# W3 of the experts in three fp32r passes throughout, with a full high part and moved inner buffers

## What is computed

```python
def hier_moe(h, w_rg, b_rg, w_re, b_re, w1, w3, w2):
    ...  # comb: weights of the two chosen experts of each token
    for g in range(N_EXPERT_GROUPS):
        a = jnp.einsum('btd,edf->btef', h, w1[g])
        b = jnp.einsum('btd,edf->btef', h, w3[g])
        hid = jax.nn.silu(a) * b * comb[:, :, g, :, None]
        out = out + jnp.einsum('btef,efd->btd', hid, w2[g])
    return out
```

## Time and profile before

| | |
|---|---|
| median of three executions | 1249.23 us (1248.32 to 1250.2) |
| the profiled execution | 1248.79 us, its span 1246.9 us |
| PE busy | 1164.0 us, 93% of the span |
| DVE busy | 706.2 us, 57% |
| ACT busy | 530.7 us, 44% |
| DMA, mean | 281 GB/s |
| experts: L1182, passes, 512 columns | 128 of each kind, 392 to 402 ns each |
| experts: L1210, fp32 products, 256 columns | 256 records (two for a product), 379 ns each, 60.5 us |
| experts: `e2Lo` splits | 32 (two in each of the 16 tiles), 2290 ns each |

### The profile page before, as it was taken

How to read it: one execution, slowest core, us unless ns; L and a number is a source line. 1 busy time by engine, 2 the same in 40 slices (tenths; PEclk the granted TensorE clock), 3 DMA queues, 4 the chain that set the end, 5 groups by cost and what they waited for, 6 DMA issues and landing times. The chain is left out here.

```text
span 1246.9 us, 21908 instructions
## 1 busy us (share of the span) xinstructions
PE 1164.0 (93%) x8635; PEld 1000.1 (80%) x8635; DVE 706.2 (57%) x1189; ACT 530.7 (43%) x744; POOL 175.1 (14%) x277
## 2 busy tenths in 40 slices
PE   3789999999999999999999999999499999999966
PEld 2678889888898998996779999998477777777742
DVE  1544655565656545553344443568777777777736
ACT  5323333232423323331244444334267676677632
POOL 0054344344443000000000000000300000000011
PEclk9799999999999999999979999999699999999997
DMA  9999878769656598648798786492599999999815
GB/s 299 322 376 354 287 265 309 272 222 319 235 171 239 202 344 280 253 154 325 278 333 292 274 282 224 122 339 70 193 353 409 404 381 376 377 367 378 314 55 190
DMA packets 172797, 350.37 MB, mean 281 GB/s; under 512 B 11347, under 2 KB 110187, under 8 KB 170630
## 3 DMA queue, kind: packets, MB, share of 16 engines
q1 hardware_dynamic: 164198, 326.35, 73.1%
q0 software_dynamic: 6304, 14.50, 3.4%
q10 hardware_dynamic: 2224, 8.52, 2.1%
HBM read 319.78 MB, written 117.65 MB: 351 GB/s over the span
## 5 line engine op out<-in xcount | busy, mean ns | idle before, releaser
L844 PE MATMUL psum<-hHi,whi 128*128 128x272 f32 x1216 | 360.8, 297 | 3.8 <-ACT rb L1378 2.0
L844 PE MATMUL psum<-hLo,whi 128*128 128x272 f32 x1216 | 353.2, 290 | 0.0
L844 PE MATMUL psum<-hHi,wlo 128*128 128x272 f32 x1216 | 351.7, 289 | 0.0
L844 PEld LDWEIGHTS psum<-hHi,whi 128*128 128x128 f32 x1216 | 231.1, 190 | 21.6 <-issue 17.8
L844 PEld LDWEIGHTS psum<-hHi,wlo 128*128 128x128 f32 x1216 | 231.2, 190 | 0.0
L844 PEld LDWEIGHTS psum<-hLo,whi 128*128 128x128 f32 x1216 | 230.7, 190 | 0.0
L1543 DVE TENSOR_TENSOR wlo<-wraw,whi 128x1024 fp32r<-128x1024 f32 x100 | 131.4, 1317 | 68.9 <-ACT whi L1292 68.4
L1292 ACT ACTIVATE whi<-wraw 128x1024 fp32r<-128x1024 f32 x100 | 104.7, 1051 | 27.0 <-PE psum L844 21.5
L2058 DVE TENSOR_TENSOR e2Lo<-e,e2Hi 128x2048 fp32r<-128x2048 f32 x32 | 73.3, 2290 | 32.7 <-ACT e2Hi L1468 31.8
L1378 ACT ACTIVATE rb<-psum 128x272 f32<-128x272 f32 x48 | 18.9, 394 | 136.7 <-PE psum L844 127.8
L2058 DVE TENSOR_TENSOR e1Lo<-e,e1Hi 128x2048 fp32r<-128x2048 f32 x30 | 68.6, 2285 | 5.7 <-ACT e1Hi L1477 4.2
(11 more groups left out here) (351 smaller groups left out, 2303.1 us busy)
## 6 DMA issues: line engine op xcount, KB each, us to landing
e<-in_w_dram SPq DMA_DIRECT2D x48, 2048.0 KB, 10.9
wraw<-in_w_in_dram SPq DMA_DIRECT2D x76, 512.0 KB, 5.1
out_dram<-in_cache_k_dram SPq DMA_DIRECT2D x32, 1022.0 KB, 8.8
out_dram<-in_cache_v_dram SPq DMA_DIRECT2D x32, 1022.0 KB, 8.0
adar<-in_w_ada_dram SPq DMA_DIRECT2D x36, 512.0 KB, 6.1
kvr<-in_cache_k_dram SPq DMA_DIRECT2D x8, 2048.0 KB, 9.4
kvr<-in_cache_v_dram SPq DMA_DIRECT2D x8, 2048.0 KB, 8.2
out_dram<-in_cache_k_dram SPq DMA_DIRECT2D x8, 1016.0 KB, 6.7
```

Source lines behind the costliest of these rows:

```text
L844: mm = pe.matmul(psum[:, t, 0:HALF], w[:, slot, k, :], x[:, k, cols], start=(k == 0 and n == 0), stop=(k == k_n - 1 and n == 2))
```

## The change

- The high part `e3Hi` gets eight blocks instead of four. ACT fills it in two copies of four blocks, one after the other, where there was one, for the first tile and in every tile's loop body.
- DVE makes `e3Lo` in two splits: both behind `xgLo` in the loop, the second one behind `xgLo` and ahead of `e2Lo` at the start. The copy to `xg32` goes, and the buffer too.
- PE makes all of B by passes: 24 of 256 columns in each half, and waits for the second split of `e3Lo` at k = 4 of half 0. The transposes of the hidden rows keep their place between k = 3 and k = 4 of half 1.
- `lo_done` and `hi_done` get six counts in a tile, so 10 becomes 12 and 5 becomes 6 in the waits.
- `sil`, `hid` and `hidHi` lie at the start of memory, where tables of the conditioning (`small` to `A2`) were; `xgHi` lies behind `xgLo`, which makes room for the larger `e3Hi`. ACT's first `e3Hi` therefore waits for `moved_act`.

```diff
@@ buffers
     e2Hi = r("e2Hi", [P, FC, D], F32R)
     xgLo = r("xgLo", [P, 2, KC, TS], F32R)
+    xgHi = r("xgHi", [P, 2, KC, TS], F32R)
+    assert r.at <= x2_at
+    r = Region(base + P * 4)
     sil = r("sil", [TS, DE])
     hid = r("hid", [TS, DE])
     hidHi = r("hidHi", [P, FC, TS], F32R)
-    assert r.at <= x2_at
+    assert r.at <= last2_at
...
-    e3Hi = r("e3Hi", [P, KC // 2, DE], F32R)
-    xgHi = r("xgHi", [P, 2, KC, TS], F32R)
-    xg32 = r("xg32", [P, 2, KC // 2, TS])
+    e3Hi = r("e3Hi", [P, KC, DE], F32R)
@@ PE
-                        pe.wait_ge(lo_done, 10 * jp + (SPLIT + 5 * q + 2 + k // 4))
+                        pe.wait_ge(lo_done, 12 * jp + (SPLIT + 6 * q + 2 + k // 4))
...
-                    for k in range(KC // 2):
-                        if half == 0 and k == 0:
-                            pe.wait_ge(lo_done, 10 * jp + (SPLIT + 5 * q + 4))
-                        passes(out, xgHi[:, q, k, :], xgLo[:, q, k, :], e3Hi[:, k, cols], e3Lo[q][:, k, cols],
-                               k == 0, False)
-                    if half == 1:
-                        pe.wait_ge(hid_done, 4 * jp + (2 * q + 3))
-                        hidden_T(0, 3)
-                    for k in range(KC // 2, KC):
-                        mm = pe.matmul(out, xg32[:, q, k - KC // 2, :], e3[q][:, k, cols], start=False,
-                                       stop=(k == KC - 1))
+                    for k in range(KC):
+                        if half == 0 and k % 4 == 0:
+                            pe.wait_ge(lo_done, 12 * jp + (SPLIT + 6 * q + 4 + k // 4))
+                        if half == 1 and k == KC // 2:
+                            pe.wait_ge(hid_done, 4 * jp + (2 * q + 3))
+                            hidden_T(0, 3)
+                        mm = passes(out, xgHi[:, q, k, :], xgLo[:, q, k, :], e3Hi[:, k, cols], e3Lo[q][:, k, cols],
+                                    k == 0, k == KC - 1)
                     mm.then_inc(b_pe, 1)
@@ ACT, ahead of the loop
             act.wait_ge(e3_in[0], 16)
-            act.activation(e3Hi[:, :, :], e3[0][:, 0:4, :], ACT.Copy).then_inc(hi_done, 1)
+            act.wait_ge(moved_act, 3)
+            for ks in (slice(0, 4), slice(4, 8)):
+                act.activation(e3Hi[:, ks, :], e3[0][:, ks, :], ACT.Copy).then_inc(hi_done, 1)
             act.wait_ge(xgT_pe, 1)
-            act.wait_ge(moved_act, 3)
@@ ACT, tile
                     act.wait_ge(b_pe, 4 * jp + (2 * q + 4))
-                    act.activation(e3Hi[:, :, :], e3[nx][:, 0:4, :], ACT.Copy).then_inc(hi_done, 1)
+                    for ks in (slice(0, 4), slice(4, 8)):
+                        act.activation(e3Hi[:, ks, :], e3[nx][:, ks, :], ACT.Copy).then_inc(hi_done, 1)
@@ DVE, ahead of the loop
-            split_lo_of(e3Lo[0][:, 0:4, :], e3[0][:, 0:4, :], e3Hi[:, :, :], SPLIT + 4)
+            split_lo_of(e3Lo[0][:, 0:4, :], e3[0][:, 0:4, :], e3Hi[:, 0:4, :], SPLIT + 4)
...
-            dve.tensor_copy(xg32[:, 0], psum[:, 4:8, 0:TS])
...
-            split_lo_of(e2Lo[0][:, 0:2, :], e2[0][:, 0:2, :], e2Hi[:, 0:2, :], SPLIT + 5)
+            split_lo_of(e3Lo[0][:, 4:8, :], e3[0][:, 4:8, :], e3Hi[:, 4:8, :], SPLIT + 5)
+            split_lo_of(e2Lo[0][:, 0:2, :], e2[0][:, 0:2, :], e2Hi[:, 0:2, :], SPLIT + 6)
@@ DVE, tile
                 dve.wait_ge(xgHi_done, 2 * jp + (q + 2))
-                dve.tensor_copy(xg32[:, nx].rearrange("p k n -> p (k n)"), psum[:, 1, 0:4 * TS])
...
-                split_lo_of(e3Lo[nx][:, 0:4, :], e3[nx][:, 0:4, :], e3Hi[:, :, :], 10 * jp + (SPLIT + 5 * q + 9))
-                split_lo_of(e2Lo[nx][:, 0:2, :], e2[nx][:, 0:2, :], e2Hi[:, 0:2, :], 10 * jp + (SPLIT + 5 * q + 10))
+                for part in range(2):
+                    ks = slice(4 * part, 4 * part + 4)
+                    split_lo_of(e3Lo[nx][:, ks, :], e3[nx][:, ks, :], e3Hi[:, ks, :], 12 * jp + (SPLIT + 6 * q + 10 + part))
+                split_lo_of(e2Lo[nx][:, 0:2, :], e2[nx][:, 0:2, :], e2Hi[:, 0:2, :], 12 * jp + (SPLIT + 6 * q + 12))
```

More of the change, by code:

```diff
@@ L121, in _build @@
     A2 = keep("A2", [P, KC, 9])
+    last2_at = keep.at
     last2 = keep("last2", [P, KC, 2 + 2 * DEC_B])
@@ L1219, in tile @@
                 for part in range(2):
-                    pe.wait_ge(lo_done, 10 * jp + (SPLIT + 5 * q + 5 + part))
+                    pe.wait_ge(lo_done, 12 * jp + (SPLIT + 6 * q + 6 + part))
                     pe.wait_ge(hidLo_done, 4 * jp + (2 * q + part + 1))
@@ L2071, in tile @@
                 nx = 1 - q
-                split_lo_of(e2Lo[q][:, 2:4, :], e2[q][:, 2:4, :], e2Hi[:, 2:4, :], 10 * jp + (SPLIT + 5 * q + 6))
+                split_lo_of(e2Lo[q][:, 2:4, :], e2[q][:, 2:4, :], e2Hi[:, 2:4, :], 12 * jp + (SPLIT + 6 * q + 7))
                 if not last:
-                    split_lo_of(e1Lo[nx][:, 0:4, :], e1[nx][:, 0:4, :], e1Hi[:, 0:4, :], 10 * jp + (SPLIT + 5 * q + 7))
+                    split_lo_of(e1Lo[nx][:, 0:4, :], e1[nx][:, 0:4, :], e1Hi[:, 0:4, :], 12 * jp + (SPLIT + 6 * q + 8))
                 dve.wait_ge(sil_done, 2 * jp + (q + 2))
@@ L2079, in tile @@
                 if not last:
-                    split_lo_of(e1Lo[nx][:, 4:8, :], e1[nx][:, 4:8, :], e1Hi[:, 4:8, :], 10 * jp + (SPLIT + 5 * q + 8))
+                    split_lo_of(e1Lo[nx][:, 4:8, :], e1[nx][:, 4:8, :], e1Hi[:, 4:8, :], 12 * jp + (SPLIT + 6 * q + 9))
                 for half in range(2):
```

## The result

| | before | changed |
|---|---|---|
| median of 17 executions each | 1249.56 us | 1252.24 us |
| range of the executions | 1244.27 to 1252.98 | 1250.36 to 1254.89 |
| span of the profiled execution | 1246.9 us | 1249.7 us |
| interval from hid1 to hid1, odd tiles (median) | 18.49 us | 18.04 us |
| the same, even tiles | 19.30 us | 20.51 us |

The ratio of the two kernels is 1.0025, 95% interval 1.0015 to 1.0035: slower by 0.25%, which is 3.1 us; the two medians of the table lie 2.7 us apart. The forecast was 1255.2 us in a range of 1251.5 to 1260.0 and slower; the direction and the range held, and the size of the change was about half of the 6.1 us that were forecast.

A forecast was written before the change was run, and what follows sets the result against it. PE was taken to bound odd tiles, the ACT-DVE chain even ones. Six even tiles +8.64, seven odd -1.61, beginning -0.5, tile 14 +0.17, tile 15 -0.54 gave 6.16 us: 1255.2 us against the median, range 1251.5 to 1260.0.

The forecast's parts named there:

- the ACT-DVE chain: ACT's copies, yev, table loads and sil, then DVE's e1Lo, hidLo and hid1; taken to set even tiles, 19.29 to 20.73 us.
- PE's part: In B, fp32r passes replace exact fp32 products: 6.45 to 5.9 us, a gain of 0.54 us where the tile waits for PE.
- ACT's part: Second e3Hi copy ahead of e2Hi: +1.90 us on ACT in each tile, 0.42 covered, so even tiles +1.44 us.
- 0.42: Even tile: 0.32 us that the second yev waits for PE plus 0.1 us overlap, taken to cover part of ACT's copy.
- by the page: The Trainium skill's 1.80 us for a 2048-column copy instead of the measured 1.90; the sum would end 0.6 us lower.
- DVE's part: Second e3Lo split of 2.2 us fits behind hid1; odd tile ends on the chain at 18.26 us, 0.23 shorter.
- Tile 14: Behind the loop's exit, without table loads: 18.26 plus 0.40 us for ACT's gap at the branch, against 18.49: +0.17 us.
- Tile 15: Last tile, with no next tile to split for, so PE's gain in B counts: -0.54 us.
- The beginning: Ahead of tile 0, its B included: second copy and split fall into waits, first xgLo starts earlier; -0.5 us (0 to -1.0).
- PE decides everywhere: Rival: the second copy is hidden and PE's 0.54 us counts in 16 tiles, giving 1240.6 us; 5%.
- the 0.99 us ahead of the table load are slack: Rival: ACT's idle gap in even tiles is an outside wait that covers 0.99 us more in six tiles, 1249.4 us; 9%.
- the rival of the clock: Rival: PE's two waits in even tiles bring its clock to 1.2 GHz, giving 1285 us; 3%.

The follow-up runs named there:

- the first four experiments: The kernel before with ACT's second copy, PE's passes or DVE's second split alone, and the changed one without ACT's second copy: ratios 1.0068, 0.9948, 1.0008, 0.9966.
- the six kernels of the later experiments: Kernels before and changed: second e1Lo split behind hid1, without or with early e3Hi copy; changed: early copy alone, or all plus xg load first: ratios 0.9925 to 0.9972.

## Why the prediction held, and where its sizes were off

**The bound.** That PE sets odd tiles and the ACT-DVE chain even ones is shown from both sides: PE's passes alone shorten only odd tiles (18.49 to 17.87), and ACT's copy alone lengthens only even ones (19.30 to 20.76).

**PE's part.** Forecast 0.54 us in B, measured 0.62 (5.83 instead of 6.45). The prediction's own terms, 4 x 1.42 + 0.17 + 0.1, add up to 5.95 us and so to a gain of 0.50, not 0.54. The way back from transposes to passes, put at 0.1 us, was nearly free: 5.83 is 4 x 1.42 and 0.15 for all that the transposes cost.

**ACT's part.** Right in its mechanism and place, too large in size: the even tile grew by 1.2 us, not 1.44, and this is the term that mattered most, six times. I took 1.90 us for a second copy from the spacing of `e3Hi` and `e2Hi` in the earlier trace rows. That spacing was not a copy's own: in both tiles `e2Hi` waited for PE's first half of Y as well. The last matmul of that half in the timeline of PE of the kernel before:

```profile
1034.33 0.40 PE L1182 MATMUL psum<-e2Hi,hidLo 128*96 128x512 f32 x1
```

It ends at 1034.73, and `e2Hi` starts at 1034.77; in the even tile the two times are 1053.21 and 1053.31. That this wait made the spacing is read from these times, no run tests it by itself. In the changed kernel, where `e2Hi` comes long behind that half, the spacing is 1.80 to 1.81 us, and the earlier trace rows had a spacing near it already, 1.82 from `e2Hi` to the first `yev`. Two copies in a row take 1.80 us each, so the chain grew by 2 x 1.80 - 1.90 = 1.70 us, and in the even tile by 2 x 1.80 - 1.94 - 0.42 = 1.24.

The Trainium skill (ScalarE: Activation LUTs, What ACT_TABLE_LOAD costs) gave an estimate of 1.80 us for this copy; the runs agree with it and not with the value I preferred to it. I also put too little on it: that the sum would end 0.6 us lower by the page counts the even tiles alone. With 0.1 us less in seven odd tiles and in tile 14 as well it would have been 1.4 lower.

So the term that was mis-sized is the second copy, 1.90 us in the sum and 1.7 in the trace. It stands in 14 tiles (six even, seven odd, tile 14), and 14 times 0.2 is 2.8 of the 3.4 us by which the sum of 6.16 exceeds the 2.8 between the spans.

**DVE's part.** That its second split is free was right (ratio 1.0008), and so was that the odd tile would end up on the chain instead of on PE: 18.04 measured, 18.26 forecast. The difference is the same error: 9.08 us from hid1 to `e2Hi` were forecast, 8.88 are measured (1033.55 to 1042.43), 1.71 more than the 7.67 of before less the 0.49 of the wait. Without ACT's copy that tile is at PE's own 17.87.

**The ends.** Tile 14 was forecast at +0.17 and came at -0.2 (18.51 to 18.28). Tile 15: -0.54 forecast, -0.6 measured. The beginning, up to hid1 of tile 2, came at +1.0 where -0.5 - 0.23 + 1.44 = +0.7 was forecast, but not for my reasons: PE waited 1.0 us for a load there,

```profile
PE psum L1172 <- DMA xg<-x_rows: 1.0, 1, 1.0
```

which the profile before does not have. With this row and those of the experiments I read the first two tiles differently now (last section). The 0.6 us that the end of the kernel behind the last hid1 is shorter were not forecast, and no run explains them; executions of one kernel differ by several microseconds.

**The sum again**, with a copy's real 1.80: even tiles 6 x 1.24, odd ones 7 x -0.45, ends as measured (-0.76 for hid1 of tile 0, 916.82 instead of 917.58, -0.2 and -0.6) give 7.4 - 3.15 - 1.6, so +2.7 us, and the spans differ by 2.8. It leaves out the 1.0 us of the wait for `xg` and the 0.6 us of the end, which take each other off in the main, so an agreement to a tenth is partly luck.

**The rivals.** That PE decides everywhere fell with PE's passes alone. That the 0.99 us ahead of the table load are slack fell with the trace of the changed kernel, where the gap is 0.99 again with the chain 1.2 us longer. The clock stayed at 1.00 through waits of 1.1 us, twice in each even tile, so the rival of the clock fell too. But the evidence that I gave against it was read too coarsely. The mean of 0.96 between 570 and 630 us hides a fall to the lower level (0.50, so 1.2 GHz) right behind the longest of those waits. The windows and the matmuls of PE of the kernel before (idle time in square brackets):

```profile
620.00:625.00 5.00, 2.58 (x24) 0.55 (x20) 4.30 (x5) 5.00 (x8) 0.00 (x0) 0.96 1.00 374
625.00:630.00 5.00, 3.25 (x17) 0.35 (x9) 2.89 (x5) 1.91 (x4) 0.00 (x0) 0.50 1.38 535
```

```profile
590.91 1.92 PE L969 MATMUL psum<-kvr,pTs 128*32 128x512 f32 x16 [1.73 <-DMA kvr<-in_cache_v_dram]
623.54 2.63 PE L969 MATMUL psum<-kvr,pTs 128*32 128x512 f32 x16 [2.42 <-DMA kvr<-in_cache_v_dram]
```

From 570 to 620 us every window of 5 us has 1.00, also behind the wait of 1.73 us. No run tests what brought the fall; it followed the wait of 2.42 us, in a kernel with such waits the rival was less remote than I made it, and a mean over 60 us was no evidence against it.

## What to carry to other kernels

Busy shares hide a bound that alternates: here PE was busy 98% of the stage, and yet every second tile was set by ACT and DVE; the intervals of one instruction from tile to tile showed it at once. Work given to an engine with 30% of idle time costs most of its price (here 1.2 of 1.8 us in every even tile) if that idle time is the wait for its own chain's result, so look where in the chain the new instruction stands, and move it, or another one that the chain doesn't need, into the wait. The spacing of two instructions is the price of the first only if nothing else released the second.

## What the runs showed that I had not expected

- The first tiles wait for loads, and an early start is lost there in part. In the kernel before, the changed one, and the first four experiments, hid1 of tile 0 lies between 911.53 and 917.58 us, 6 us apart, but hid1 of tile 2 between 954.62 and 957.03: whoever comes early has tiles 1 and 2 of up to 22.5 us. ACT and PE wait for loads there (in the changed kernel without ACT's second copy ACT waits 1.9 us for W3 and 3.0 for W2). It is no fixed bound: in the six kernels of the later experiments hid1 of tile 2 lies between 949.71 and 958.22 us.
- A kernel with shorter tiles can run into its own loads without a sign of it in the GB/s. With tiles of 18.3 us on average a 2 MB load lands 16.2 us after its issue instead of 10.3, and 0.4 MB issued ahead of W3's 2 MB instead of behind them changed ACT's waits for weights from 3.4 to 31 us. That loads would bound a kernel with still shorter tiles is likely by this, but no run shows it.
